# Handing x from one sublayer to the next in a two-layer trunk: z scaled on its way out of PSUM, outputs multiplied by ScalarE, two first tiles begun together with the squares summed between them

## The reference, cut to what matters

```python
def layer(x, c, l):                    # x: 512 prompt tokens and 32 sample tokens, 1024 wide
    mods = silu(c) @ w_ada[l] + b_ada[l]      # shift, scale, gate for each of three sublayers
    x = gated_post(x, swiglu(modulated_pre(x, ..., 0)), ..., 0)      # ffn0, 1024 -> 2816 -> 1024
    h = modulated_pre(x, ..., 1)
    z = h @ w_in[l]            # latents of attention (q 256, kv 128, rope 32), retention q, k, v, g
    x = gated_post(x, concat(mla(z), retention(z)) @ w_out[l], ..., 1)    # the mixer
    x = gated_post(x, swiglu(modulated_pre(x, ..., 2)), ..., 2)      # ffn1
    return x
def modulated_pre(x, g, mods, j):      # rms_norm(x) = x * rsqrt(mean(x^2) + eps)
    return rms_norm(x, g) * (1 + mods[:, 3*j+1]) + mods[:, 3*j]
def gated_post(x, o, g, mods, j, coef):
    return x + coef * mods[:, 3*j+2] * rms_norm(o, g)
```

## Time and profile before

| | |
|---|---|
| median of 3 runs | 2654.85 us (2653.37 to 2655.97) |
| the profiled execution | 2653.0 us, span 2650.9 us |
| mean granted TensorE clock | 0.964 of 2.4 GHz |
| PE busy | 2403.4 us, 91% of the span |
| DVE busy | 1274.3 us, 48% |
| ACT busy | 891.6 us, 34% |
| POOL busy | 869.0 us, 33% |

### The profile page before, as it was taken

How to read it: one execution, slowest core, us unless ns; L and a number is a source line. 1 busy time by engine, 2 the same in 40 slices (tenths; PEclk the granted TensorE clock), 3 DMA queues, 4 the chain that set the end, 5 groups by cost and what they waited for, 6 DMA issues and landing times.

```text
span 2650.9 us, 46339 instructions
## 1 busy us (share of the span) xinstructions
PE 2403.4 (91%) x17558; PEld 2246.0 (85%) x17558; DVE 1274.3 (48%) x2040; ACT 891.6 (34%) x1308; POOL 869.0 (33%) x366
## 2 busy tenths in 40 slices
PE   1999989699888899999979999987988898999996
PEld 1999989599456799999979999987974587999996
DVE  7333388845463333237252335895725515233562
ACT  2434321333233433332243433223333334443321
POOL 0334334243100433434423333442420033333443
PEclk9999999899899899999989999998999998999998
DMA  6222277223100122226312224751220011222461
GB/s 215 73 86 87 93 244 260 80 80 119 42 5 1 64 72 87 87 92 247 113 49 87 83 83 159 276 186 56 87 85 32 1 41 49 85 87 87 163 212 55
DMA packets 71514, 272.52 MB, mean 103 GB/s; under 512 B 8640, under 2 KB 10048, under 8 KB 70528
## 3 DMA queue, kind: packets, MB, share of 16 engines
q1 hardware_dynamic: 71424, 271.35, 30.0%
HBM read 267.87 MB, written 3.45 MB: 102 GB/s over the span
## 4 chain that ended last, share of the span: by engine, by line
PE 64%; issue 20%; DVE 9%; POOL 4%; ACT 2%; DMA 1%; DVEq 1%; POOLq 0%; ACTq 0%; SPq 0%
PE ps L501 18%; PE ps L502 18%; PE ps L505 18%; POOL w_lo L437 3%; DVE wide_v L1271 2%; PE ps L765 2%; PE ps L809 2%; PE ps L761 1%; PE ps L511 1%; DVE wide_rinv L1215 1%; DVE wide_v L1184 1%; PE ps L675 1%; DVE ret_st L1403 1%; DMA raw<-in_w_mix 1%; DVE x L1264 1%
## 5 line engine op out<-in xcount | busy, mean ns | idle before, releaser
L437 POOL TENSOR_TENSOR w_lo<-raw,w_hi 128x1024 fp32r<-128x1024 f32 (+1 forms) x304 | 789.7, 2599 | 1649.5 <-ACT w_hi L881 1371.6
L501 PE MATMUL ps<-h_hi,w_hi 128*128 128x274 f32 (+1 forms) x3488 | 953.0, 290 | 20.6 <-DVE h_lo L1226 20.3
L502 PE MATMUL ps<-h_lo,w_hi 128*128 128x274 f32 (+1 forms) x3488 | 953.7, 291 | 0.0
L505 PE MATMUL ps<-h_hi,w_lo 128*128 128x274 f32 (+1 forms) x3488 | 727.1, 290 | 0.0
L501 PEld LDWEIGHTS ps<-h_hi,w_hi 128*128 128x128 f32 x3488 | 665.0, 191 | 26.5 <-DVE h_lo L1226 25.4
L502 PEld LDWEIGHTS ps<-h_lo,w_hi 128*128 128x128 f32 x3488 | 659.9, 189 | 0.4
L881 ACT CAST w_hi<-raw 128x1024 fp32r<-128x1024 f32 (+1 forms) x244 | 277.0, 1135 | 848.3 <-PE ps L505 629.9
L505 PEld LDWEIGHTS ps<-h_hi,w_lo 128*128 128x128 f32 x3488 | 552.4, 189 | 0.0
L501 PE MATMUL ps<-u_hi,w_hi 128*128 128x272 f32 x1408 | 384.1, 292 | 15.8 <-POOL w_lo L437 15.8
L502 PE MATMUL ps<-u_lo,w_hi 128*128 128x272 f32 x1408 | 381.3, 289 | 0.0
L1184 DVE CUSTOM_DVE_ANT_0 wide_v<-ada_w,ps 128x1024 bf16<-128x1024 f32 x288 | 332.0, 1217 | 46.6 <-DMA ada_w<-in_ada 18.5
...
## 6 DMA issues: line engine op xcount, KB each, us to landing
...
```

Source lines behind the costliest of these rows:

```text
L437: pool.tensor_tensor(w_lo[:, slot, 0:width], raw[:, slot, 0:width], w_hi[:, slot, 0:width].bitcast(F32), ALU.subtract).then_inc(lo_done.se ...
L501: pe.matmul(ps[:, bank + t, 0:half], wh, hi[:, n], start=start, stop=False)
L502: pe.matmul(ps[:, bank + t, 0:half], wh, lo[:, n], start=False, stop=False)
L505: last = pe.matmul(ps[:, bank + t, 0:half], wl, hi[:, n], start=False, stop=stop)
```

## The change

1. **Mixer by pre_scale.** The mixer's begin is that of an ffn. z tiles are 274 wide. A z tile leaves PSUM by DVE times 1/root (`z_scaled`, L1348 of the changed kernel, into the buffer z_tmp), then ACT adds the shift by its bias (prompt and sample columns apart: two activations in place of one). PE's next tile in the same banks waits for DVE's product. The five first z tiles use banks 0, 2, 4, 2, 0, and z_scaled stands between DVE's other work (latent reciprocals, rope).
2. **Output tiles.** ACT squares a tile first, then copies it by three activations times mul_post (272, 240 and 32 columns). mul_post is made earlier on DVE, after two ada groups.
3. **Post-norm.** The reciprocal is written to PSUM (banks 4 and 5). DVE multiplies 544 columns by one instruction, and adds. POOL has the next sublayer's first two w_lo ahead of its three additions, not behind them.
4. **First tiles.** PE takes the first two tiles together: per step k the 8 matmuls that need h_hi alone, and then the 32 of h_lo; the sums of squares stand between them, from step 4 on. ACT scales three tiles ahead of squaring them.
5. **Loops.** The layer loop is written out on all engines, and the first feature pair of `up` stands ahead of its loop.

```diff
# POOL
+            def turn_over(l, j, chunk):
+
+                for k in range(2):
+                    low(l, chunk + k, k, KD * P)
+                if l or j:
+                    for m in range(1, KD - 1, 2):
+                        add_odd(*((l, j - 1) if j else (l - 1, 2)), m)
+                for k in range(2):
+                    low(l, chunk + 2 + k, k, KD * P)
# PE
+            def first_tiles(l, j, chunk):
+
+                for k in range(KD):
+                    pe.wait_ge(h_high.sem, h_high.at(l, H_AT[j] + 2 + 2 * k + 2))
+                    for w in range(2):
+                        if k == 0:
+                            pe.wait_ge(lo_done.sem, lo_done.at(l, chunk + w + 1))
+                        for t in range(2):
+                            n = slice(t * HW, (t + 1) * HW)
+                            pe.matmul(ps[:, 2 * w + t, 0:HW], w_hi[:, w, k * P:(k + 1) * P], h_hi[:, k, n],
+                                      start=k == 0, stop=False)
+                            pe.matmul(ps[:, 2 * w + t, 0:HW], w_lo[:, w, k * P:(k + 1) * P], h_hi[:, k, n],
+                                      start=False, stop=False)
+                    if k >= 4:
+                        pre_sum(l, j, k - 4)
+                for w in range(2):
+                    for k in range(KD):
+                        if w == 0:
+                            pe.wait_ge(h_ready.sem, h_ready.at(l, H_AT[j] + 2 + 2 * k + 2))
+                        for t in range(2):
+                            n = slice(t * HW, (t + 1) * HW)
+                            last = pe.matmul(ps[:, 2 * w + t, 0:HW], w_hi[:, w, k * P:(k + 1) * P], h_lo[:, k, n],
+                                             start=False, stop=k == KD - 1)
+                        if w == 0 and k % 2:
+                            if k == KD - 1:
+                                last.then_inc(w_used.sem, 1)
+                            pre_sum(l, j, 4 + k // 2)
+                last.then_inc(w_used.sem, 1)
+
+            def pre_sum(l, j, m):
+                pe.wait_ge(x_sq.sem, x_sq.at(l, j * KD + m + 1))
+                add_squares(tmp_s[:, m % 2, :], 6, m == 0, m == KD - 1, ones).then_inc(sums.sem, 1)
...
# ACT, begin of a sublayer
-                for k in range(2):
-                    high(l, next_chunk + k, k, KD * P)
-                for m in range(KD):
-
+                high(l, next_chunk + 1, 1, KD * P)
+
+                def scaled(m):
                     act.wait_ge(x_new[m % 2].sem, x_new[m % 2].at(l, (j - 1) * (KD // 2) + m // 2 + 1))
-                    act.wait_ge(sums.sem, sums.at(l, j * (KD + 1) + m - 1))
-                    nc.scalar.activation(tmp_s[:, m % 2, :], x[:, m, :], ACT.Square).then_inc(x_sq.sem, 1)
                     for v, n in enumerate((slice(0, NP_), slice(NP_, T))):
                         nc.scalar.activation(h_hi[:, m, n], x[:, m, n], ACT.Copy,
                                              scale=mul_pre[:, j, v, m:m + 1]).then_inc(h_high.sem, 1)
+
+                def squared(m):
+                    act.wait_ge(sums.sem, sums.at(l, j * (KD + 1) + m - 1))
+                    nc.scalar.activation(tmp_s[:, m % 2, :], x[:, m, :], ACT.Square).then_inc(x_sq.sem, 1)
+
+                for m in range(3):
+                    scaled(m)
+                for m in range(3, KD):
+                    scaled(m)
+                    squared(m - 3)
+                for m in range(KD - 3, KD):
+                    squared(m)
+                high(l, next_chunk + 2, 0, KD * P)
                 act.wait_ge(sums.sem, sums.at(l, j * (KD + 1) + KD))
                 root_of(l, rooted, 2 * j, 6, D)
+                high(l, next_chunk + 3, 1, KD * P)
...
# ACT, end of a sublayer, and z tiles
                     act.wait_ge(w_used.sem, w_used.at(l, chunk0 + (m + 1) * per_tile))
-                    o_tile = o_buf[:, bass.ds(m, 1), :].rearrange("p a (t n) -> p (a t) n", t=2)
-                    nc.scalar.copy(o_tile, pair(2 * mm)).then_inc(out_ev.sem, 1)
                     act.wait_ge(sq_added.sem, sq_added.at(l, j * (KD - 1) + m - 1))
                     nc.scalar.activation(halves(tmp_s[:, mm, :]), pair(2 * mm), ACT.Square).then_inc(out_sq.sem, 1)
-
-                with act.Fori(0, KD // 2 - 1) as i:
+                    act.wait_ge(columns.sem, columns.at(l, (6, COL_A, COL_A + 6)[j]))
+                    for t in range(2):
+                        n = NP_ - t * HT if t else HT
+                        nc.scalar.activation(o_buf[:, m, t * HT:t * HT + n], ps[:, 2 * mm + t, 0:n], ACT.Copy,
+                                             scale=mul_post[:, j, 0, m:m + 1])
+                    nc.scalar.activation(o_buf[:, m, NP_:T], ps[:, 2 * mm + 1, NP_ - HT:HT], ACT.Copy,
+                                         scale=mul_post[:, j, 1, m:m + 1]).then_inc(out_ev.sem, 1)
...
-                def z_out(z, bank, dst, func=ACT.Copy):
-                    act.wait_ge(w_used.sem, w_used.at(l, MIX_C0 + z + 1))
-                    nc.scalar.activation(dst, pair(bank), func).then_inc(z_ev.sem, 1)
+                pre_scale(l, 1, MIX_C0)
+
+                def z_out(z, buf, dst, func=ACT.Identity):
+                    act.wait_ge(z_mul.sem, z_mul.at(l, z + 1))
+                    nc.scalar.activation(dst[:, 0:NP_], z_tmp[:, buf, 0:NP_], func, bias=z_tmp[:, buf, T:T + 1])
+                    nc.scalar.activation(dst[:, NP_:T], z_tmp[:, buf, NP_:T], func, bias=z_tmp[:, buf, T + 2:T + 3])\
+                        .then_inc(z_ev.sem, 1)
...
# DVE
+            def turn_over(post, pre):
+
+                if post is not None:
+                    l, j, o_buf = post
+                    dve.wait_ge(rooted.sem, rooted.at(l, 2 * j + 2))
+                    v_.reciprocal(out_inv, halves(root[:, :])).then_inc(inverted.sem, 1)
+                    dve.wait_ge(inverted.sem, inverted.at(l, 2 * j + 2))
+                    dve.wait_ge(out_ev.sem, out_ev.at(l, (j + 1) * KD))
+                    for m in range(KD):
+                        if m >= 2:
+
+                            dve.wait_ge(x_new[m % 2].sem, x_new[m % 2].at(l, j * (KD // 2) + m // 2))
+                        v_.tensor_tensor(halves(tmp_v[:, m % 2, :]), halves(o_buf[:, m, :]), out_inv, ALU.mult)\
+                            .then_inc(x_prod.sem, 1)
+                        if m % 2 == 0 or m == KD - 1:
+                            dve.wait_ge(x_prod.sem, x_prod.at(l, j * KD + m + 1))
+                            v_.tensor_tensor(x[:, m, :], x[:, m, :], tmp_v[:, m % 2, :], ALU.add)\
+                                .then_inc(x_new[m % 2].sem, 1)
+                if pre is not None:
+                    l, j = pre
+                    dve.wait_ge(columns.sem, columns.at(l, COL_A if j else 0))
+                    dve.wait_ge(h_high.sem, h_high.at(l, H_AT[j] + 2))
+                    for v in range(2):
...
+                def z_scaled(z):
+                    dve.wait_ge(w_used.sem, w_used.at(l, MIX_C0 + z + 1))
+                    dve.wait_ge(inverted.sem, inverted.at(l, 3))
+                    if z >= 2:
+                        dve.wait_ge(z_ev.sem, z_ev.at(l, z - 1))
+                    bank = (0, 2, 4, 2, 0)[z] if z < Z_EARLY else 2 * (z % 2)
+                    v_.tensor_tensor(halves(z_tmp[:, z % 2, :]), wide_pair(bank), halves(wide_rinv[:, :]), ALU.mult)\
+                        .then_inc(z_mul.sem, 1)
+
+                def invert_latent(n):
+                    dve.wait_ge(m_root.sem, m_root.at(l, n + 1))
+                    v_.reciprocal(root[:, :], root[:, :]).then_inc(m_inv.sem, 1)
+                    dve.wait_ge(m_inv.sem, m_inv.at(l, n + 1))
 
                 v_.tensor_copy(gains[:, :], g_lat[:, bass.ds(l * 3, 3)]).then_inc(gains_in.sem, 1)
+                for z in range(4):
+                    z_scaled(z)
+                invert_latent(0)
+                z_scaled(4)
                 dve.wait_ge(gains_in.sem, gains_in.at(l, 1))
-                invert(l, m_root, m_inv, 0)
                 for k in range(2):
...
                         turn(tmp_s[:, 1, :], a2, sin, ALU.mult)
                         turn(tmp_v[:, 0, :], a1, sin, ALU.mult)
                         turn(tmp_v[:, 1, :], a2, cos, ALU.mult)
+                        z_scaled(9 + 4 * g + (2 if t is ret_k else 0))
                         dve.wait_ge(rope.sem, rope.at(l, turns[0]))
                         for hh in range(4):
                             r = slice(32 * hh, 32 * hh + 32)
                             pair_tile, row = 2 * g + hh // 2, 64 * (hh % 2)
                             turn(t[row:row + 32, pair_tile, :], tmp_s[r, 0, :], tmp_s[r, 1, :], ALU.subtract)
                             turn(t[row + 32:row + 64, pair_tile, :], tmp_v[r, 1, :], tmp_v[r, 0, :], ALU.add)
+                        z_scaled(10 + 4 * g + (2 if t is ret_k else 0))
+                for z in range(17, Z_C):
+                    z_scaled(z)
                 dve.wait_ge(uq_ev.sem, uq_ev.at(l, 8))
```

275 lines of the change are left out of this document (112 added, 163 removed).

## The result

| | before | after |
|---|---|---|
| median | 2654.11 us (2651.52 to 2655.97, 4 runs) | 2585.39 us (2583.01 to 2587.24, 4 runs) |
| ratio to before | | 0.9741 (95% interval 0.9724 to 0.9758) |
| the profiled execution | 2653.0 us, span 2650.9 | 2585.33 us, span 2583.3 |
| mean granted TensorE clock | 0.964 | 0.978 |
| DVE busy | 1274.3 us | 1308.3 us |

The change takes 68.7 us off the median; 61.9 were forecast from the profile. The time lies in the range, 7.6 us under the forecast of 2593.

The account below looks back on a forecast made before the run. PE, busy 91% of the span, was taken to lose time at the five handovers of x. Gains of 9.2, 9.2, 9.6, 15.3, 16.5, 1.2 and 0.9 sum to 61.9, giving 2593 us (forecast 2585 to 2603; full range 2576 to 2616).

Parts of the forecast that it names:

- The x chain: DVE and POOL forming x at a handover: complete 11.6 us after the post-norm reciprocal in place of 17.5, the stall gone.
- the first tiles: PE's first two tiles at a handover: both done at r + 24.3, if PE's clock is high.
- the 0.45: Post-norm's root comes 0.45 us later than before, since three activations follow the last output tile's squaring.
- r: The time at which the reciprocal of the post-norm ends at a handover; 488.18 us in ffn0 to mixer of layer 0.
- Rival A: z stage bound by DVE, still held up by POOL: 22 us less gained, 21 with what comes back; about 2614; chance 0.18.
- Rival C: Gaps keep PE at 1.2 GHz into the first tiles: 17.5 us more per handover, 2680 us; chance 0.03.
- The lag of the z stage: Mixer z tiles: PE waits for z_scaled among DVE's rope turns, 5.5 us late at the end, between 3.1 and 8.1.
- To an ffn: Handover from mixer to ffn: second tile leaves at 25.3 us after r instead of 34.5, a gain of 9.2 per layer.
- taken as nothing because two chunks are already in place: ACT's wait for mul_post in ffn1, with the next w_hi behind it: between 0 and 5 us each, counted as nothing.
- The start with ffn0: Start of the kernel: both first tiles overlap the squaring, a gain of 0.9 us, between 0 and 2.
- I take nothing, between a gain of 5 and a loss of 5: Layer loop written out: more instructions to load, no jump back; counted as zero, within 5 us either way.
- The mixer of layer 1: Handover to that mixer: z tile 20 ends at r + 149.45, root's delay included, instead of 166.0; a gain of 16.5 us.

## Why the prediction came out as it did

**Right, step by step.** The x chain (10.84 for 11.6; POOL's addition and the products met even less), the first tiles (24.4 for 24.3), z tile 20 (147.5 and 148.4 for 149.0 with the 0.45 not counted), a z tile at 6.1 us (541.91 to 566.34 for four). In the first tiles two things offset each other. x came 0.8 us early, and tile 7 was scaled at r + 14.2 all the same; the terms that I gave for that (two scalings and a squaring behind 11.6) make only 13.8. ACT's squarings wait for PE's sums, and PE has no gaps by then, so x was hardly what PE waited for. The root is 0.39 later behind PE's last product (3.63 us to the reciprocal; before, 3.24 in five of the six sublayers), forecast 0.45. Rival A is out: L1269 and L1348 never take over 0.73 us. Rival C is out: PE starts at 1.2 GHz in every handover but is at 2.4 GHz 3.3 to 6.3 us later.

**The lag of the z stage** was put too high. PE's waits for z_scaled are 2.7 us per mixer, where I had put a lag of 5.5 within 3.1 to 8.1. 12 turns with two z_scaled take 13.47 us (571.68 to 585.15 on DVE), not 14.3, mostly since one of the two turns that meet POOL takes 2.28 us and not 2.81.

**Mis-sized, down.** To an ffn I put 9.2. Its first tiles gained 10.1 (34.48 against 24.39), and 3.2 were given back before the next r in layer 0 (2.8 in layer 1): 0.6 by the w_lo of chunk 2 and 0.4 by the root, both forecast, and 1.7 (1.3) by "taken as nothing because two chunks are already in place". That step failed: ACT's wait for mul_post does reach PE, at 1.7 us, within the bounds I had kept (0 to 5). The 0.5 that is left I can't place.

**Mis-sized, up.** The start with ffn0 gained 4.8 where I had 0.9. 1.6 are the first tiles (their second product leaves at 77.1 instead of 78.7), 3.5 are shorter waits for w_lo in the down projection (9.6 us before, 6.1 after). The step that failed is "I take nothing, between a gain of 5 and a loss of 5" for the loops. The run with the loops alone shows 5 us and a start with ffn0 that is 5.5 shorter. Of these 2.0 are shorter waits for w_lo (9.6 to 7.6), and 1.2 lie ahead of the first tiles (the first reciprocal at 66.87, not 68.10). That DVE frees the ada ring earlier, and w_dn comes earlier by it, is my reading and was not tested; against it, the same waits in ffn0 of layer 1 are not shorter in the changed kernel (6.2 us before, 6.5 after). The mixer of layer 1 gained 4.4 more than forecast: 0.5 before z tile 20 (17.5 for 17.0, the root not counted) and 3.9 behind it, where the forecast had only the root's loss of 0.45. Two windows of attention, before and (same distance from z tile 20) after:

```profile
2063.78:2083.78 20.00, 16.15 (x77) 10.42 (x76) 13.85 (x29) 7.49 (x21) 0.00 (x0) 0.92 0.01 2
2103.78:2123.78 20.00, 17.62 (x90) 12.86 (x91) 5.49 (x16) 3.36 (x11) 0.00 (x0) 0.91 0.00 0
```

```profile
2008.53:2028.53 20.00, 16.31 (x90) 10.81 (x89) 14.24 (x30) 7.48 (x21) 0.00 (x0) 1.00 0.00 1
2048.53:2068.53 20.00, 18.33 (x101) 12.30 (x99) 7.56 (x24) 5.58 (x17) 0.00 (x0) 1.00 0.00 1
```

PE was at 0.92 and 0.91 of its clock there, and is at 1.00 after. In layer 0 of the kernel before the same windows are at 1.00. In the kernel with POOL's order alone, whose attention is the same, it is layer 0 that has a dip there (0.91 in 773.99 to 793.99), and layer 1 has none. So the dips come and go from one mixer and one execution to the next, and I count them as no gain of the change; at 0.08 to 0.09 of 20 us each, the two would make some 3 us at most (an estimate from these rows). Two profiled executions can differ by that in a stage that nobody touched. In layer 0 the mixer gained 1.4 more than forecast up to z tile 20 (17.2 for 15.8, the root not counted) and lost 1.0 behind it, 0.4 of which are the root's.

**Luck in the total.** The gains of the seven stages miss the forecast by +3.9, +0.9, -2.3, +0.3, +4.4, -1.9 and +0.5 us. They make 5.8 together, and the time stands at the very edge of the bounds that I gave the forecast (2585 to 2603). Without the clock of one mixer it would have been some 3 us nearer, so the mechanism carried the forecast, but its closeness rests in part on misses of both signs.

**The parts are not additive.** Alone, POOL's order gives 18 us, the mixer's part and the loops 31, the loops by themselves 5. Undone from the whole, POOL's order costs 59 and the joint first tiles 49, which is together more than the whole change of 69. Each of w_lo, h_hi and a tile that needs only these must be there for PE to start at r + 2.5; without the w_lo it starts at r + 11.8, without such a tile at r + 11.9 (h_hi was not taken away by itself). My schedule had that (its sum was for the whole list), but my expectations for the single undone parts were too low by a factor of 1.3 to 2.
